# Three groups of weight units multiplied in pairs of ring slots, 512 columns a pass

## The chip, the cores and the metric

The kernel runs on one core of one Trainium2 chip. The metric is the device time in microseconds of one execution of the whole program, lower is better. Before the change it is 1397.33 us, the median of 3 runs (1395.53 to 1398.47).

## The reference

The reference is a small network on one sequence of 256 tokens with 1024 features, in float32. It has two parts, run one after the other.

The first part has two layers. Layer 0 is a sparse attention: a projection, an index score that picks 64 keys for each query, a softmax over the picked keys, an output projection. Layer 1 is a gated linear attention (GLA): `proj = x @ w_in` is split into q, k, v, r and a narrow gate input; the log decay is summed within chunks of 64 tokens; the output is the part within a chunk, from decayed q times k, plus a part from a running state. Behind each comes a layer norm, an MLP of 4096 hidden features with a squared ReLU, and a layer norm.

The second part projects its normed input to the inputs of four branches. One is a differential attention (a_q, a_k, a_v), one a forgetting attention (f_q, f_k, f_v), one a causal convolution of 31 taps, one a short convolution. Each is multiplied by its own branch matrix and gated, the sum goes through an output matrix, and a cross attention to a second input and a feed-forward block with a 3-tap convolution follow.

All that matters for the change are three of the projections: v of the GLA layer (1024 columns), a_v (512 columns) and f_v (512 columns). Each is `x @ w`, with x of 256 tokens by 1024 features.

## The kernel before

**Units and the ring.** All large weights are cut into 183 units of 128 partitions by 2048 floats (1 MB), in the order of their use (`UNITS`). GLA's v is `gv`, units 48 to 51; a_v is `av`, units 96 and 97; f_v is `fv`, units 102 and 103. A ring of `RING` = 4 slots holds them, unit u in slot u % 4. SyncE's queue loads a unit into `raw`. ScalarE copies it, rounded to the fp32r type, into `whi` (`high_part`, L906). VectorE writes the remainder into `wlo` (`low_part`, L1307). A product is then three matmuls into the same PSUM bank, high by high, high by low and low by high (`three`, L422 to L424). TensorE may begin a unit when its low part is there (`arrived`).

**Activations.** The input of a projection lies as features by tokens, in high and low parts `xh` and `xl`: 8 blocks of 128 features, 256 tokens each.

**Two kinds of unit.** In most units (`unit_up`) the weights are the stationary operand and the 256 tokens stream. For v-like projections (`unit_tok`, L463) the result is wanted as tokens by features, so the tokens are stationary and the weights stream. A unit holds 256 output features: for each half `t` of the tokens and each of the 8 feature blocks, three matmuls stream 256 columns of the unit, in all 48 matmuls. Both halves go into one bank `lin`, 256 columns each.

**Order and waits.** Each result bank has a number, a job, given out by `plan()`. `LAST[u]` is the last job that reads unit u. `bank(j)` waits until job j - 4 has been copied out of its bank. `high_part(u)` waits for the transfer of unit u and for job `LAST[u - 4]`. ScalarE's and VectorE's programs are written out in order. ScalarE's `copy(name, i, ...)` is `high_part` of the unit three further on (`AHEAD` = 3), a wait for the job, and the copy out of the bank (L921). VectorE's `next_low(name, i)` is `low_part` of the unit three further on.

**Around gv.** In front of gv TensorE computes the gate's low-rank input and the gate (L672, L679). ScalarE and VectorE turn that into the log decay and its running sum `bcum` (L1582 to L1590). VectorE's program then is:

```
            next_low("gv", 0)
            next_low("gv", 1)
            level_args(0)
            link(v.memset(attnD[:], 0.0))
            next_low("gv", 2)
            next_low("gv", 3)
            ...
            for l in range(6):
                level_pairs(l)
```

The product within a chunk is built in 7 levels. For each, VectorE makes the arguments (`level_args`, L1604 and L1605), ScalarE the exponential (`level_decay`, L1075), VectorE the decayed q and k (`level_pairs`, L1615), TensorE the product (`level`, L694), VectorE the sum. The units of `gr` are put between the levels on TensorE. Then come the transposes of k (L707), the states (L723) and the output.

**Around av and fv.** TensorE's order is aq, a narrow product, ak, av, fq, fk, fv, then c and s with steps of the two attentions between the units, all `unit_up` but av and fv. VectorE makes only low parts from ak to fv. From the first unit of s on it also computes the 31 taps of the convolution (L1746, L1748).

Of the kernel before, what the change touches and what calls it, by code (L numbers as in the profile page):

```python
# [17 lines left out]
P = 128  # L18
S = 256
D = 1024  # L20
DB = D // P
RING = 4
UT = 16
UW = UT * P
# [30 lines left out]
COUNT = dict(UNITS)  # L55
U0 = {}
# [10 lines left out]
def plan():  # L67


    job, last, n = {}, {}, [0]  # L70

    def add(name, i=0, unit=None, banks=1):
        job[name, i] = n[0]
        n[0] += banks
        if unit:
            last[U0[unit] + i] = n[0] - 1

    def units(name, count, banks=1):
        for i in range(count):
            add(name, i, name, banks)  # L80

    def norm(name, mean=False):
        if mean:
            add(name + "_mean")
        add(name + "_sq"); add(name + "_rstd")

    units("iq", 2); add("ik"); add("iw"); add("rope", 0); add("rope", 1); add("rope", 2)
    units("k", 1); units("v", 1); add("rope", 3)
    for i in range(6):
        add("idx", i)  # L90
    units("q", 4)
    for i in range(4):
        add("rope", 4 + i)
    units("ao", 4); norm("ln0", True)
    for layer in range(2):
        for half in range(2):
            units(f"up{layer}{half}", 8); units(f"dn{layer}{half}", 8)
        norm(f"ln{2 * layer + 1}", True)
        if layer == 0:
            units("gq", 2); units("gk", 2); add("alow"); add("gate_a", 0); add("gate_a", 1)  # L100
            units("gv", 4)
            for l in range(7):
                if l in GLA_FILL:
                    add(*GLA_FILL[l], GLA_FILL[l][0])
                add("level", l)
            add("gr", 2, "gr"); add("kd", 0); add("kd", 1); add("state", 0); add("state", 1)
            for i in range(4):
                add("gla_o", i)
            add("gr", 3, "gr")
            add("gla_sq"); add("gla_rstd", 0); add("gla_rstd", 1)  # L110
            units("go", 4); norm("ln2", True)
    norm("pre_mix")
    units("aq", 2); add("fg")
    for name in ("ak", "av", "fq", "fk", "fv", "c", "s"):
        units(name, COUNT[name])
    add("gate0", 0, "gate0"); add("gate0", 1, "gate0"); add("ya_sq"); add("gate0", 2, "gate0"); add("ya_rstd", 0); add("ya_rstd", 1)
    add("gate0", 3, "gate0"); units("br0", 2, 2); units("gate3", 4); units("br3", 2, 2)
    add("gate1", 0, "gate1"); add("gate1", 1, "gate1"); add("conv_mean"); add("gate1", 2, "gate1"); add("conv_sq")
    add("gate1", 3, "gate1"); add("conv_rstd"); units("br1", 2, 2); units("gate2", 4); units("br2", 2, 2)
    add("out", 0, "out"); add("out", 1, "out"); add("mem_sq"); add("out", 2, "out"); add("mem_rstd"); add("out", 3, "out")  # L120
    add("xk", 0, "xk"); add("post_mix_sq"); add("xk", 1, "xk"); add("post_mix_rstd"); add("xv", 0, "xv"); add("pre_x_sq"); add("xv", 1, "xv"); add("pre_x_rstd"); units("xq", 2); units("xo", 2, 2)
    norm("post_x"); norm("pre_ffn")
    units("fu", FB)
    for i in range(DB):
        add("fd", i)
    for u in range(COUNT["fd"]):
        last[U0["fd"] + u] = job["fd", (UT * u + UT - 1) // FB]
    norm("post_ffn")
    return job, last


JOB, LAST = plan()


# [47 lines left out]
def build(nc, units_d, x_d, mem_d, pos_d, vec_d, const_d, narrow_a_d, narrow_b_d, narrow_f_d, w_a2_d, b_fgt_d, lam_d, out_d):  # L182
    f32, f32r = mybir.dt.float32, mybir.dt.float32r
    i32 = mybir.dt.int32
    ACT, AX = mybir.ActivationFunctionType, mybir.AxisListType
    ctx = ExitStack()
    with ctx:
# [3 lines left out]
        def sbuf(name, shape, dt=f32, where=ctx):  # L191
            return where.enter_context(nc.sbuf_tensor(name, shape, dt))


        raw = [sbuf(f"raw{i}", [P, UW]) for i in range(RING)]
        whi = [sbuf(f"whi{i}", [P, UW], f32r) for i in range(RING)]
        wlo = [sbuf(f"wlo{i}", [P, UW], f32r) for i in range(RING)]
        h = sbuf("h", [P, DB, S])
        z = sbuf("z", [P, DB, S])
        xh = sbuf("xh", [P, DB, S], f32r)  # L200
# [210 lines left out]
        def _(pe):  # L411
# [41 lines left out]
            def unit_down(u, j, first, g=None):  # L453
# [6 lines left out]
                    last = three(o[:, 0, :], tile(u, k), (fh[:, k, :], fl[:, k, :]), k == 0, k == UT - 1)  # L460
                last.then_inc(job_done, 1)

            def unit_tok(u, j):  # L463

                arrived(u)
                o = bank(j)
                for t in range(2):
                    for k in range(DB):
                        at = slice(t * P, (t + 1) * P)
                        last = three(o[:, t, :], (xh[:, k, at], xl[:, k, at]), tile(u, 2 * k, 2), k == 0, k == DB - 1)  # L470
                last.then_inc(job_done, 1)
# [203 lines left out]
            for i in range(2):  # L675
# [2 lines left out]
                    hd = 2 * i + n  # L678
                    last = mm(o[:, n, :], w_a2[:, hd * P:(hd + 1) * P], alow[:], start=True, stop=True)  # L679
                last.then_inc(job_done, 1)  # L680
            for i in range(4):
                unit_tok(U0["gv"] + i, JOB["gv", i])

            def level(l):

# [76 lines left out]
                last = mm(o[0:8, 0, :], narrow_f[:, k, :], z[:, k, :], start=k == 0, stop=k == DB - 1)  # L762
            last.then_inc(job_done, 1)
            ups("ak")
            for i in range(2):
                unit_tok(U0["av"] + i, JOB["av", i])
            for name in ("fq", "fk"):
                ups(name)
            for i in range(2):
                unit_tok(U0["fv"] + i, JOB["fv", i])  # L770
            fill = [("c", i) for i in range(4)] + [("s", i) for i in range(6)]
            for s, (name, i) in enumerate(fill):
                unit_up(U0[name] + i, JOB[name, i])
# [117 lines left out]
        def _(act):  # L891
# [7 lines left out]
            def high_part(u, g=None, used=None):  # L899

                if u >= NU:
                    return
                act.wait_ge(raw_full[u % RING], per(16 * (u // RING + 1), g, 16))
                if u >= RING:
                    act.wait_ge(job_done, per(LAST[u - RING] + 1 if used is None else used, g, RING))
                f(whi[u % RING][:], raw[u % RING][:], ACT.Copy).then_inc(hi_ready, 1)  # L906

            def unit(name, i):

# [3 lines left out]
            def passed(name):  # L913

                for i in range(COUNT[name]):
                    high_part(U0[name] + i + AHEAD)

            def copy(name, i, dst, scale=1.0):
                unit(name, i)
                j = JOB[name, i]  # L920
                f(dst, lin[j % RING][:], ACT.Copy, scale=scale).then_inc(evac[j % RING], 1)  # L921
# [153 lines left out]
                f(decay[:], gtmp[:], ACT.Exp, scale=1.0 / 16).then_inc(lvl_exp, 1)  # L1075

            for i in range(4):
                copy("gv", i, gv_tok[:, :, i * S:(i + 1) * S])
                if i == 1:
                    level_decay(0)  # L1080
            for l in range(6):
# [47 lines left out]
            for i in range(2):  # L1129
                copy("ak", i, two(akT, i))  # L1130
            for i in range(2):
                copy("av", i, av_tok[:, :, i * S:(i + 1) * S])
            for name, dst in (("fq", fqT), ("fk", fkT)):
                for i in range(2):
                    copy(name, i, two(dst, i))
            for i in range(2):
                copy("fv", i, fv_tok[:, :, i * S:(i + 1) * S])

            def branch_split(n, src, ready):

# [143 lines left out]
        def _(dve):  # L1284
# [18 lines left out]
            def low_part(u, g=None):  # L1303

                if u < NU:
                    dve.wait_ge(hi_ready, per(u + 1, g, RING))
                    v.tensor_tensor(wlo[u % RING][:], raw[u % RING][:], whi[u % RING][:].bitcast(f32), ALU.subtract).then_inc(lo_ready, 1)  # L1307

            def next_low(name, i=None):

# [729 lines left out]
```

## Time and profile before

| | |
|---|---|
| median of the runs | 1397.33 us |
| the profiled execution, its own time | 1394.16 us |
| its span, first to last instruction | 1392.3 us |
| TensorE (PE) busy | 95% |
| VectorE (DVE) busy | 67% |
| ScalarE (ACT) busy | 45% |
| mean granted TensorE clock | 0.967 of full speed |

Times of the rows are microseconds from the start of the span. Matmuls are pipelined: each lasts longer than the distance to the next, so the distance between starts, and not the duration, is what one costs in a stream. PE is a matmul, PEld the load of its weights. A bracket at the end of a timeline row is the time that the engine idled before it, and what ended that. In a plain float32 product each matmul of the program appears as two records; in an fp32r product it is one.

### The profile page before, as it was taken

The numbers are of one execution on the slowest core, as the hardware profiler recorded it, in microseconds if no ns is written. First come the engines' busy times: TensorE is split into PE (matmuls) and PEld (weight loads), VectorE is DVE, ScalarE is ACT, GpSimd is POOL, SyncE is SP. The second block draws the span as 40 slices with busy tenths as digits, with TensorE's granted clock in tenths as the row PEclk, the third lists the DMA queues.
The fourth block names the chain that finished last, engine by engine and source line by source line (L and its number), as shares of the span: only waits on it lengthen the run. The fifth ranks groups of instructions, "written<-read, shape, count | busy, mean of one in ns | idle before, by whom it ended". The sixth has DMA issues, their size and how long they took to land.

```text
span 1392.3 us, 25125 instructions
## 1 busy us (share of the span) xinstructions
PE 1326.4 (95%) x10604; PEld 1272.3 (91%) x10604; DVE 928.1 (67%) x1448; ACT 627.4 (45%) x805; POOL 0.2 (0%) x4
## 2 busy tenths in 40 slices
PE   6889999999998899999999999999899999999897
PEld 6866999999998799999999999889898989999797
DVE  6783576466647767646665458888876665999943
ACT  5334454354444244534435444454445455555431
POOL 0000000000000000000000000000000000000000
PEclk9975999999999899999999999999999999999999
DMA  8320325545334133554532543334445241444430
GB/s 330 115 91 0 122 104 198 184 178 191 115 122 152 61 121 105 198 184 179 195 138 94 209 159 120 118 127 150 141 172 203 92 152 61 152 181 157 175 121 31
DMA packets 28361, 198.41 MB, mean 142 GB/s; under 512 B 3296, under 2 KB 3808, under 8 KB 4592
## 3 DMA queue, kind: packets, MB, share of 16 engines
q1 hardware_dynamic: 27072, 194.00, 38.7%
q10 hardware_dynamic: 1200, 3.14, 0.6%
q8 instruction: 66, 1.08, 0.3%
q14 instruction: 23, 0.19, 0.0%
HBM read 196.08 MB, written 1.05 MB: 142 GB/s over the span
## 4 chain that ended last, share of the span: by engine, by line
PE 69%; DVE 23%; ACT 3%; issue 3%; DMA 1%; DVEq 0%; ACTq 0%
PE lin L422 19%; PE lin L424 18%; PE lin L423 18%; DVE wlo L1307 7%; DVE conv L1748 3%; PE lin L504 2%; PE att L589 2%; PE att L497 2%; DVE fconv L1922 1%; PE att L556 1%; ACT whi L906 1%; PE att L573 1%; DVE fconv L1921 1%; DVE fconv L1923 1%; PE lin L527 1%
## 5 line engine op out<-in xcount | busy, mean ns | idle before, releaser
L422 PE MATMUL lin<-xh,whi 128*128 128x256 f32 x1936 | 556.2, 287 | 17.2 <-DVE xl L1317 11.8
L1307 DVE TENSOR_TENSOR wlo<-raw,whi 128x2048 fp32r<-128x2048 f32 x183 | 418.7, 2291 | 215.2 <-ACT whi L906 214.0
L423 PE MATMUL lin<-xl,whi 128*128 128x256 f32 x1936 | 550.8, 284 | 0.0
L424 PE MATMUL lin<-xh,wlo 128*128 128x256 f32 x1936 | 550.5, 284 | 0.0
L906 ACT ACTIVATE whi<-raw 128x2048 fp32r<-128x2048 f32 x183 | 348.5, 1906 | 179.5 <-PE lin L424 172.7
L422 PEld LDWEIGHTS lin<-xh,whi 128*128 128x128 f32 x1936 | 375.0, 194 | 21.4 <-DVE wlo L1307 10.6
L423 PEld LDWEIGHTS lin<-xl,whi 128*128 128x128 f32 x1936 | 375.0, 194 | 0.1
L424 PEld LDWEIGHTS lin<-xh,wlo 128*128 128x128 f32 x1936 | 374.5, 193 | 0.0
L422 PE MATMUL lin<-fh,whi 128*128 128x256 f32 x512 | 143.4, 280 | 0.0
L423 PE MATMUL lin<-fl,whi 128*128 128x256 f32 x512 | 142.8, 279 | 0.0
L424 PE MATMUL lin<-fh,wlo 128*128 128x256 f32 x512 | 142.8, 279 | 0.0
L424 PEld LDWEIGHTS lin<-fh,wlo 128*128 128x128 f32 x512 | 96.3, 188 | 0.0
L422 PEld LDWEIGHTS lin<-fh,whi 128*128 128x128 f32 x512 | 96.1, 188 | 0.0
L423 PEld LDWEIGHTS lin<-fl,whi 128*128 128x128 f32 x512 | 95.8, 187 | 0.0
L1748 DVE SCALAR_TENSOR_TENSOR conv<-upad,vec,conv 128x256 f32<-128x256 f32 x120 | 58.1, 484 | 3.9
L497 PE MATMUL att<-consts 128*128 128x128 f32 x464 | 57.0, 275 | 0.0
L422 PE MATMUL lin<-gh,whi 128*128 128x256 f32 x176 | 50.7, 288 | 6.4 <-DVE gl L1937 6.4
L497 PEld LDWEIGHTS att<-consts 128*128 128x128 f32 x464 | 54.6, 192 | 0.4 <-issue 0.2
L973 ACT ACTIVATE pr<-lg,nmax 128x128 f32<-128x128 f32 (+1 forms) x72 | 32.4, 452 | 48.5 <-DVE nmax L1436 43.5
L422 PE MATMUL lin<-whi,xh 128*128 128x256 f32 x176 | 50.7, 288 | 0.0
L423 PE MATMUL lin<-wlo,xh 128*128 128x256 f32 x176 | 50.5, 287 | 0.0
L424 PE MATMUL lin<-whi,xl 128*128 128x256 f32 x176 | 50.5, 287 | 0.0
(309 smaller groups left out, 1645.5 us busy)
## 6 DMA issues: line engine op xcount, KB each, us to landing
raw<-units_dram SPq DMA_DIRECT2D x183, 1024.0 KB, 4.8
h<-x_dram SPq DMA_DIRECT2D x1, 1024.0 KB, 6.8
memT<-mem_dram ACTq DMA_DIRECT2D x1, 1024.0 KB, 4.8
out_dram<-h SPq DMA_DIRECT2D x4, 256.0 KB, 2.0
consts<-consts_dram ACTq DMA_DIRECT2D x1, 867.5 KB, 12.2
narrow_a<-narrow_a_dram ACTq DMA_DIRECT2D x1, 544.0 KB, 14.1
vec<-vectors_dram ACTq DMA_DIRECT2D x1, 245.5 KB, 16.9
posi<-pos_dram ACTq DMA_DIRECT2D x1, 128.0 KB, 8.0
```

The lines of the kernel that those rows point to most:

```text
L422: mm(out, w[0], a[0], start=first, stop=False)
L423: mm(out, w[0], a[1], start=False, stop=False)
L424: return mm(out, w[1], a[0], start=False, stop=last)
L497: mm(att[0][:, 0:P], ident, ident, start=True, stop=True)
L504: ins = mm(flat[:, (col + t) * width:(col + t + 1) * width], block[:, t * P:(t + 1) * P], ones[:, 0:width], start=first and t == 0, stop=l ...
L527: last = mm(o[:, n, t * P:(t + 1) * P], inv[:, col:col + 1].broadcast_to([P, P]), ident, start=True, stop=True)
L556: last = mm(o, qT[r, i // 2, q], keys[r, i // 8, 0:w], start=True, stop=True)
L589: last = mm(o, v, pT[u % 2][:, n, :], start=b == 0, stop=b == att_keys(u, m) // P - 1)
L906: f(whi[u % RING][:], raw[u % RING][:], ACT.Copy).then_inc(hi_ready, 1)
L973: last = f(pr[u % 2][:, m, 0:w], lg[u % 2][:, m, 0:w], ACT.Exp, scale=-1.0, bias=nmax[:, u % 2, m:m + 1], accum_out=rsum[:, u % 2, m:m + 1])
L1307: v.tensor_tensor(wlo[u % RING][:], raw[u % RING][:], whi[u % RING][:].bitcast(f32), ALU.subtract).then_inc(lo_ready, 1)
L1748: ins = v.scalar_tensor_tensor(out=conv[:, b, :], in0=x, scalar=w, in1=conv[:, b, :], op0=ALU.mult, op1=ALU.add)
```

## The change

`unit_tok` for gv, av and fv becomes `units_tok`, which takes two neighbouring units at once. The slots of `whi` and of `wlo` become one tensor each, so that an operand can reach over two slots. For each half of the tokens, the 256 columns of the one unit and the 256 of the other stream in one matmul of 512 columns into a bank of its own. The bank of job j holds the first half of the tokens and 512 features, that of job j + 1 the second half. In `plan()` both units of a pair have the second job as their last. ScalarE copies a bank into the tensor of its half of the tokens. The units `v` and `xv` stay with `unit_tok`.

```diff
--- before.py
+++ after.py
@@ -79,6 +79,11 @@
         for i in range(count):
             add(name, i, name, banks)
+    def tokens(name, count):
+        for i in range(0, count, 2):
+            add(name, i); add(name, i + 1)
+            last[U0[name] + i] = last[U0[name] + i + 1] = n[0] - 1
+
     def norm(name, mean=False):
         if mean:
             add(name + "_mean")
@@ -98,7 +103,7 @@
         norm(f"ln{2 * layer + 1}", True)
         if layer == 0:
             units("gq", 2); units("gk", 2); add("alow"); add("gate_a", 0); add("gate_a", 1)
-            units("gv", 4)
+            tokens("gv", 4)
             for l in range(7):
                 if l in GLA_FILL:
                     add(*GLA_FILL[l], GLA_FILL[l][0])
@@ -112,7 +117,10 @@
     norm("pre_mix")
     units("aq", 2); add("fg")
     for name in ("ak", "av", "fq", "fk", "fv", "c", "s"):
-        units(name, COUNT[name])
+        if name in ("av", "fv"):
+            tokens(name, 2)
+        else:
+            units(name, COUNT[name])
     add("gate0", 0, "gate0"); add("gate0", 1, "gate0"); add("ya_sq"); add("gate0", 2, "gate0"); add("ya_rstd", 0); add("ya_rstd", 1)
     add("gate0", 3, "gate0"); units("br0", 2, 2); units("gate3", 4); units("br3", 2, 2)
     add("gate1", 0, "gate1"); add("gate1", 1, "gate1"); add("conv_mean"); add("gate1", 2, "gate1"); add("conv_sq")
@@ -193,8 +201,10 @@
         raw = [sbuf(f"raw{i}", [P, UW]) for i in range(RING)]
-        whi = [sbuf(f"whi{i}", [P, UW], f32r) for i in range(RING)]
-        wlo = [sbuf(f"wlo{i}", [P, UW], f32r) for i in range(RING)]
+        whi_ring = sbuf("whi", [P, RING, UW], f32r)
+        wlo_ring = sbuf("wlo", [P, RING, UW], f32r)
+        whi = [whi_ring[:, i, :] for i in range(RING)]
+        wlo = [wlo_ring[:, i, :] for i in range(RING)]
         h = sbuf("h", [P, DB, S])
         z = sbuf("z", [P, DB, S])
         xh = sbuf("xh", [P, DB, S], f32r)
@@ -460,6 +470,19 @@
                     last = three(o[:, 0, :], tile(u, k), (fh[:, k, :], fl[:, k, :]), k == 0, k == UT - 1)
                 last.then_inc(job_done, 1)
+            def units_tok(u, j):
+
+
+                for n in range(2):
+                    arrived(u + n)
+                at = u % RING
+                for t in range(2):
+                    o = bank(j + t)
+                    for k in range(DB):
+                        q, cols = slice(t * P, (t + 1) * P), slice(2 * k * P, (2 * k + 2) * P)
+                        last = three(o[:], (xh[:, k, q], xl[:, k, q]), (whi_ring[:, at:at + 2, cols], wlo_ring[:, at:at + 2, cols]), k == 0, k == DB - 1)
+                    last.then_inc(job_done, 1)
+
             def unit_tok(u, j):
                 arrived(u)
@@ -678,8 +701,8 @@
                     hd = 2 * i + n
                     last = mm(o[:, n, :], w_a2[:, hd * P:(hd + 1) * P], alow[:], start=True, stop=True)
                 last.then_inc(job_done, 1)
-            for i in range(4):
-                unit_tok(U0["gv"] + i, JOB["gv", i])
+            for i in (0, 2):
+                units_tok(U0["gv"] + i, JOB["gv", i])
             def level(l):
@@ -762,12 +785,10 @@
                 last = mm(o[0:8, 0, :], narrow_f[:, k, :], z[:, k, :], start=k == 0, stop=k == DB - 1)
             last.then_inc(job_done, 1)
             ups("ak")
-            for i in range(2):
-                unit_tok(U0["av"] + i, JOB["av", i])
+            units_tok(U0["av"], JOB["av", 0])
             for name in ("fq", "fk"):
                 ups(name)
-            for i in range(2):
-                unit_tok(U0["fv"] + i, JOB["fv", i])
+            units_tok(U0["fv"], JOB["fv", 0])
             fill = [("c", i) for i in range(4)] + [("s", i) for i in range(6)]
             for s, (name, i) in enumerate(fill):
                 unit_up(U0[name] + i, JOB[name, i])
@@ -903,7 +924,7 @@
                 act.wait_ge(raw_full[u % RING], per(16 * (u // RING + 1), g, 16))
                 if u >= RING:
                     act.wait_ge(job_done, per(LAST[u - RING] + 1 if used is None else used, g, RING))
-                f(whi[u % RING][:], raw[u % RING][:], ACT.Copy).then_inc(hi_ready, 1)
+                f(whi[u % RING], raw[u % RING][:], ACT.Copy).then_inc(hi_ready, 1)
             def unit(name, i):
@@ -914,6 +935,10 @@
                 for i in range(COUNT[name]):
                     high_part(U0[name] + i + AHEAD)
+
+            def two_tok(t, i):
+
+                return t[:, i % 2, 512 * (i // 2):512 * (i // 2) + 512].rearrange("p (a s) -> p a s", s=S)
             def copy(name, i, dst, scale=1.0):
                 unit(name, i)
@@ -1075,7 +1100,7 @@
                 f(decay[:], gtmp[:], ACT.Exp, scale=1.0 / 16).then_inc(lvl_exp, 1)
             for i in range(4):
-                copy("gv", i, gv_tok[:, :, i * S:(i + 1) * S])
+                copy("gv", i, two_tok(gv_tok, i))
                 if i == 1:
                     level_decay(0)
             for l in range(6):
@@ -1129,12 +1154,12 @@
             for i in range(2):
                 copy("ak", i, two(akT, i))
             for i in range(2):
-                copy("av", i, av_tok[:, :, i * S:(i + 1) * S])
+                copy("av", i, two_tok(av_tok, i))
             for name, dst in (("fq", fqT), ("fk", fkT)):
                 for i in range(2):
                     copy(name, i, two(dst, i))
             for i in range(2):
-                copy("fv", i, fv_tok[:, :, i * S:(i + 1) * S])
+                copy("fv", i, two_tok(fv_tok, i))
             def branch_split(n, src, ready):
@@ -1304,7 +1329,7 @@
                 if u < NU:
                     dve.wait_ge(hi_ready, per(u + 1, g, RING))
-                    v.tensor_tensor(wlo[u % RING][:], raw[u % RING][:], whi[u % RING][:].bitcast(f32), ALU.subtract).then_inc(lo_ready, 1)
+                    v.tensor_tensor(wlo[u % RING], raw[u % RING][:], whi[u % RING].bitcast(f32), ALU.subtract).then_inc(lo_ready, 1)
             def next_low(name, i=None):
```

## Rows read from the trace of the kernel before

**Rows 1.** The page, part 1: busy time of each engine.

```profile
PE 1326.4 (95%) x10604; PEld 1272.3 (91%) x10604; DVE 928.1 (67%) x1448; ACT 627.4 (45%) x805; POOL 0.2 (0%) x4
```

**Rows 2.** The page, part 4: the chain that ended last, by engine.

```profile
PE 69%; DVE 23%; ACT 3%; issue 3%; DMA 1%; DVEq 0%; ACTq 0%
```

**Rows 3.** The chain of waits in 760 to 816 us, by line.

```profile
by line: PE lin L422 33.4%; PE lin L424 33.2%; PE lin L423 33.0%; PE att L559 0.8%
```

**Rows 4.** Timeline, ScalarE, av: start, duration, instruction, idle before and its releaser.

```profile
769.05 0.60 ACT L921 ACTIVATE gate<-lin 128x512 f32<-128x512 f32 x1 [3.36 <-PE lin L424]
...
774.81 0.60 ACT L921 ACTIVATE gate<-lin 128x512 f32<-128x512 f32 x1 [3.36 <-PE lin L424]
```

**Rows 5.** The chain of waits in 740 to 960 us: start, duration, piece.

```profile
841.42 0.45 PE att L559 x4
...
843.50 0.42 DVE conv L1746
```

**Rows 6.** Timeline, TensorE, from gv's first matmul on.

```profile
404.05 0.39 PE L422 MATMUL lin<-whi,xh 128*128 128x256 f32 x1
...
404.39 0.27 PE L424 MATMUL lin<-whi,xl 128*128 128x256 f32 x1
404.50 0.28 PE L422 MATMUL lin<-whi,xh 128*128 128x256 f32 x1
...
405.57 0.41 PE L423 MATMUL lin<-wlo,xh 128*128 128x256 f32 x1
...
408.13 0.41 PE L423 MATMUL lin<-wlo,xh 128*128 128x256 f32 x1
```

**Rows 7.** Timeline, TensorE, two of the GLA levels.

```profile
430.50 1.15 PE L694 MATMUL lin<-qk 128*64 128x64 f32 x32 [1.68 <-DVE qk L1615]
...
442.48 1.93 PE L694 MATMUL lin<-qk 128*64 128x64 f32 x32 [3.80 <-DVE qk L1615]
```

**Rows 8.** The chain of waits in 396 to 500 us.

```profile
429.16 1.28 DVE qk L1615 x2
...
460.47 3.68 PE lin L694 x64
```

**Rows 9.** Timeline, VectorE, gv and the first levels.

```profile
416.04 4.49 DVE L1307 TENSOR_TENSOR wlo<-raw,whi 128x2048 fp32r<-128x2048 f32 x2
...
424.74 4.50 DVE L1307 TENSOR_TENSOR wlo<-raw,whi 128x2048 fp32r<-128x2048 f32 x2 [1.92 <-ACT whi L906]
429.16 0.68 DVE L1615 TENSOR_TENSOR qk<-gkT,decay 128x512 f32<-128x512 f32 x1
...
438.20 2.29 DVE L1307 TENSOR_TENSOR wlo<-raw,whi 128x2048 fp32r<-128x2048 f32 x1 [2.92 <-ACT whi L906]
```

**Rows 10.** Timeline, TensorE, two groups of plain fp32 matmuls with what follows them.

```profile
24.55 3.61 PE L606 MATMUL lin<-h,narrow_a 128*128 128x256 f32 x16
28.00 0.62 PE L611 MATMUL lin<-narrow_a,h 128*128 128x8 f32 x5
...
491.71 3.68 PE L504 MATMUL lin<-consts,z 128*128 128x64 f32 x32
495.23 0.89 PE L497 MATMUL att<-consts 128*128 128x128 f32 x6
```

**Rows 11.** Timeline, VectorE, low parts of units 97 and 98.

```profile
759.49 4.50 DVE L1307 TENSOR_TENSOR wlo<-raw,whi 128x2048 fp32r<-128x2048 f32 x2 [1.38 <-ACT whi L906]
```

**Rows 12.** Timeline, ScalarE, gv: high parts of 51, 52, 54 and 55, copy of 49.

```profile
410.92 1.90 ACT L906 ACTIVATE whi<-raw 128x2048 fp32r<-128x2048 f32 x1
...
413.20 1.90 ACT L906 ACTIVATE whi<-raw 128x2048 fp32r<-128x2048 f32 x1
417.35 0.60 ACT L921 ACTIVATE gv_tok<-lin 128x512 f32<-128x512 f32 x1 [2.24 <-PE lin L424]
...
425.02 1.90 ACT L906 ACTIVATE whi<-raw 128x2048 fp32r<-128x2048 f32 x1
...
436.27 1.89 ACT L906 ACTIVATE whi<-raw 128x2048 fp32r<-128x2048 f32 x1
```

## The prediction

> **What bounds the kernel now.** I read the page first. TensorE has matmuls in flight for 95% of the span, and the chain that ended last is 69% TensorE and 23% VectorE [rows 1, 2]. That is an average, so the second view is the timeline around each place that the diff touches, and the two kinds of place differ.
>
> Around av and fv the chain of waits is matmuls alone, 99.6% of it on the three lines of `three` [rows 3]. ScalarE copies one result after another at 769.05 and 774.81, each time after 3.36 us of idling for TensorE [rows 4]: 5.76 us a unit, over 48 matmuls 0.120 us each. TensorE is the bound, and what it saves there is carried on. The chain stays with TensorE until 841.42 and then goes to VectorE's convolution taps, which start after an attention step that TensorE releases [rows 5]. A TensorE that is earlier at 815 therefore brings the taps forward too.
>
> Around gv it is different. TensorE has matmuls in flight from 404.05 [rows 6] to 428.8, but behind them VectorE runs the GLA levels, and TensorE waits for it: 1.68 us before the first level, 3.80 us before a later one [rows 7]. From 429.16 on the chain is VectorE and ScalarE; TensorE takes it over only at 460.47 [rows 8]. So in that stage the VectorE work that starts at 429.16 [rows 9] sets the end.
>
> **The change, part by part.**
>
> *Streaming.* For 8 units, 384 matmuls of 256 columns become 192 of 512. The columns stay the same, half of the weight loads go. What is a pass of 512 worth? No 512-column matmul of this type is in the trace, so I bound it. At the full clock 256 columns take 0.120 us. At the low clock (1.2 GHz) twelve of them take 408.13 - 405.57 = 2.56 us, 0.2133 each, which is 256 columns at 1.2 GHz and nothing over [rows 6]. So at 2.4 GHz streaming needs 0.1067, and 0.0133 comes from elsewhere. A cost added to every matmul would show at the low clock too; a floor under it would not. Two plain-fp32 groups speak for a floor of the weight load: 32 matmuls of 64 columns with 128-column weights come every (495.23 - 491.71) / 32 = 0.110 us although they stream half as long as the others, and 16 that stream 256 columns at half rate (0.2133 of streaming) come every (28.00 - 24.55) / 16 = 0.2156 [rows 10]. A load of 128 weight columns is hidden behind 0.21 us of streaming but for 0.002. A 512-column pass streams for just as long. I take 0.2156: 48 x (2 x 0.120 - 0.2156) = 1.17 us less for each pair at the full clock. The ends: 0.2133 (streaming alone, 1.28 a pair) and 0.240 (no gain); a load that is serial after all gives 0.2267 (0.64).
>
> The Trainium skill, "TensorE: Matmul & The Clock Gate" (Back-to-back issue gap), gives N / 2.4 + 2.5 ns for a matmul by itself. For 512 columns it is 215.8 ns, and rows 10 agree. For 256 columns it is 109.2 ns, and the trace disagrees with 120. By the page alone a pair would save 48 x (218.4 - 215.8) ns = 0.12 us, and the change would have next to no gain; the measured 0.120 decides.
>
> *av and fv.* Two pairs, 2 x 1.17 = 2.3 us off the path, if nothing new is waited for. The first matmul of a pair now needs both units. For av the second unit's low part is the first of the two that start at 759.49 and take 4.50 together: ready at 761.8, wanted at 763.3 (one unit before 769.05), so no wait [rows 4, 11]. For fv the margin is wider: ScalarE makes the high part of a unit right behind the copy of the unit four before it. Both ring slots come free at the pair's end instead of one in its middle; ScalarE then has two high parts (1.90 each) and a copy before the next unit's 5.76 us are over, and the unit after next is the first that needs one. So no matmul waits. VectorE's low part behind fv may reach into the first attention step; it lies beside the next unit's 5.76 us of TensorE, and uncovered it would cost its 2.29 us once. -2.3.
>
> *gv, first pair* (units 48, 49). It starts at 404.05 as now; both are ready. The low clock holds for about 3.4 us of it, where a wide pass gains nothing. Of 96 matmuls about 80 run at the full clock: 40 x 0.0244 = 1.0 us less. Unit 49's copy starts at 417.35 now [rows 12], so the pair ends at 416.4.
>
> *gv, second pair* (units 50, 51). It needs the low part of 51. That is the first of two at 416.04, 2.25 us: 418.3 [rows 9]. VectorE comes to it from the gate's chain, and 51's high part was long made (410.92 + 1.90 [rows 12]), so TensorE's speed doesn't move it. Today unit 50 fills that time. Now TensorE stands still from 416.4 to 418.4, about 2.0 us, and gives back all of the first pair's gain and more. The pair then takes 48 x 0.2156 + 0.3 (first gap and tail) = 10.65 us: 429.0, where unit 51 ends at 428.8 now.
>
> *The ring.* High part of unit u waits for the last matmul on unit u - 4. For 52 that was unit 48's end, now the first pair's: ScalarE starts it at 416.5 instead of 413.20 and VectorE's low part of 52 begins 0.2 us later. Small. For 54 it was unit 50's end, which let ScalarE start at 425.02 [rows 12]; now it is the second pair's, 429.1. Its high part ends at 431.0. And VectorE's program has the low part of 54 in front of `level_pairs(0)`: everything of the levels is queued behind it. Low part 431.1 to 433.3, and the first level starts at 433.3 instead of 429.16: **+4.1 us** on the chain that sets this stage.
>
> Is that absorbed further on? VectorE idles 2.92 us before its low part at 438.20 [rows 9], which looks like slack. It waits there for ScalarE's high part at 436.27, which comes straight behind a `decay` that waits for VectorE's own level arguments [rows 9, 12]: the wait moves with the chain. TensorE idles some 5.5 us before level 0 instead of 1.68, which costs it the clock as the 3.80 us at 442.48 did (32 matmuls of a level in 1.93 us there, 1.15 at 430.50 [rows 7]). About 0.8 us there and up to 1.7 in the unit behind; both have room beside VectorE. +4.1 stays.
>
> *Sum.* +4.1 - 2.3 = +1.8 us. On the profiled execution's own 1394.16 us that is 1396.0. The median of the runs shown is 3.2 us above that execution, so I put it on the median: 1397.33 + 1.8 = 1399.1.
>
> **The rivals.**
>
> *A, no faster streaming.* What holds 256 columns at 0.120 is the feed of the moving operand (0.469 ns a column), not the weight load. Then 512 take 0.240. For it: at the low clock a feed of that rate would be hidden as well, and fp32's floor (0.110) is not quite 0.120. Against it: a burst's first matmuls come closer than 0.120 (404.39 to 404.50 [rows 6]). Price: no gain at av and fv; gv's first pair still waits out 418.4, the second ends at 418.4 + 11.52 + 0.3 = 430.2, the levels start at 434.5. +5.3: 1402.6, slower. Each pass of the second pair, of av and of fv counts, 144 in all, so it decides from 0.2225 on (1.8 + 144 x 0.0069 = 2.8 us, which is 0.2%). The serial load (0.2267) lies between: 1.8 + 144 x 0.0111 = +3.4: 1400.7.
>
> *B, the clock falls in the new stall.* 2.0 us of standing still at 416.4. For it: the clock is at half by 405.57 although TensorE had matmuls from 404.05 on [rows 6]. Against it: after 1.68 us of idling at 430.50 the level ran at full clock [rows 7], while 3.80 us did cost it. At half clock for 3.4 us the second pair takes 1.7 us more: +3.5, 1400.8.
>
> *C, the delay of unit 54 does not reach the end.* Then only av and fv are left: -2.3, 1395.0. For it: VectorE has idle time in the level stage. Against it: each of those waits ends at ScalarE work that follows VectorE's own. Since 2.3 us is 0.16%, it too would hardly be told from no change.
>
> **How the numbers follow.** A measurement of this kernel tells 0.2% (2.8 us) from no change, hardly less. Chances: forecast 0.56 (1399.1, give or take 1.0, from where the low-clock stretches fall), A 0.17 and the serial load 0.05, B 0.09, C 0.13. Slower by over 0.2%: A, most of B and of the serial load (0.11), and 0.08 of the forecast's upper side: 0.36. Faster by over 0.2%: a part of C, 0.06. The rest, 0.58, within. The range reaches from C to A: 1395.0 to 1402.8.
>
> **What would show it.** Right: the 192 wide passes start every 0.215 to 0.217 us; TensorE idles about 2 us between the gv pairs, ended by the low part of 51; ScalarE's high part of 54 starts after gv's last matmul; VectorE's first level starts some 4 us later against the start of gv, and TensorE idles over 5 us before level 0; from ak to c the time shrinks by 2.3 us. Wrong: passes every 0.240 (A); wide passes at half clock behind the stall (B); the stretch from gv's first matmul to the `state` matmuls no longer than before (C); or any new wait in front of av or fv.

## The result, and the profile after

The changed kernel takes 1399.82 us (median of 20 runs, 1397.27 to 1404.37), the kernel before 1395.81 us (20 runs, 1392.27 to 1398.47). The ratio is 1.0029, interval [1.0022, 1.0037]: slower by 4.0 us, with 3.1 to 5.2 from the interval. The prediction said 1399.1 and +1.8. That the time was met to 0.7 us is luck: the three runs shown before lay 1.5 us above the median of twenty. The direction and the place held; the difference was over twice as large.

On the page little tells the two apart but the count of matmuls: 192 fewer, in nearly the same busy time [rows 1, 2].

```profile
PE 1327.2 (95%) x10412; PEld 1263.2 (90%) x10412; DVE 927.9 (66%) x1448; ACT 627.7 (45%) x805; POOL 0.2 (0%) x4
...
PE 70%; DVE 23%; ACT 3%; issue 3%; DMA 1%; DVEq 0%; ACTq 0%
```

The timeline of TensorE around gv (`three` is now L432 to L434, the level L717) answers to [rows 6, 7]:

```profile
405.83 0.50 PE L432 MATMUL lin<-whi,xh 128*128 128x512 f32 x1
...
416.62 0.39 PE L434 MATMUL lin<-whi,xl 128*128 128x512 f32 x1
420.22 0.47 PE L432 MATMUL lin<-whi,xh 128*128 128x512 f32 x1 [3.21 <-DVE wlo L1332]
...
421.71 0.63 PE L434 MATMUL lin<-whi,xl 128*128 128x512 f32 x1
...
423.85 0.63 PE L433 MATMUL lin<-wlo,xh 128*128 128x512 f32 x1
...
425.09 0.39 PE L434 MATMUL lin<-whi,xl 128*128 128x512 f32 x1
...
432.57 0.39 PE L434 MATMUL lin<-whi,xl 128*128 128x512 f32 x1
438.55 1.76 PE L717 MATMUL lin<-qk 128*64 128x64 f32 x27 [5.59 <-DVE qk L1640]
```

Three things are to be seen. The stall between the pairs is there and is ended by the low part of unit 51. Behind it the clock falls: from 421.71 to 423.85 five passes take 2.14 us, 0.428 each. The windows of the same stretch (from and to, length, TensorE busy and count, granted clock, DMA share, GB/s) show it directly:

```profile
417.00:420.22 3.22, 0.01 (x1) 1.00 0.00 0
420.22:421.30 1.08, 1.08 (x5) 0.91 0.38 68
421.30:424.30 3.00, 3.00 (x9) 0.50 0.93 336
```

At the full clock 33 passes take 432.57 - 425.09 = 7.48 us, 0.2267 each: not 0.2156. ScalarE (its high parts are L927) answers to [rows 12], VectorE (low parts L1332, first level L1640) to [rows 9]:

```profile
417.10 1.91 ACT L927 ACTIVATE whi<-raw 128x2048 fp32r<-128x2048 f32 x1 [2.01 <-PE lin L434]
...
433.06 1.91 ACT L927 ACTIVATE whi<-raw 128x2048 fp32r<-128x2048 f32 x1 [4.90 <-PE lin L434]
```

```profile
417.83 4.49 DVE L1332 TENSOR_TENSOR wlo<-raw,whi 128x2048 fp32r<-128x2048 f32 x2
...
426.52 2.29 DVE L1332 TENSOR_TENSOR wlo<-raw,whi 128x2048 fp32r<-128x2048 f32 x1 [1.92 <-ACT whi L927]
435.00 2.29 DVE L1332 TENSOR_TENSOR wlo<-raw,whi 128x2048 fp32r<-128x2048 f32 x1 [6.18 <-ACT whi L927]
437.21 0.69 DVE L1640 TENSOR_TENSOR qk<-gkT,decay 128x512 f32<-128x512 f32 x1
```

High parts of 52 and 54 start as TensorE ends a pair. Before, the low parts of 53 and 54 were one row of 4.50 us. Now 6.18 us of idling stand between them, and the first level is queued behind the second.

Since the two executions differ by 1.78 us already where gv starts, stages are compared by distances. The columns are: first gv matmul to VectorE's first level; from there to the first `state` matmul; first narrow product behind aq to the first logits of the second part (this holds av and fv); from there to the end of the span; gv's first matmul to the end. Each is a difference of starts in the timelines.

| kernel | to first level | levels | av, fv | rest | gv to end | ratio to before |
|---|---|---|---|---|---|---|
| before | 25.11 | 43.90 | 67.08 | 577.33 | 988.29 | 1 |
| changed | 31.38 | 42.98 | 65.84 | 577.34 | 992.36 | 1.0029 [1.0022, 1.0037] |
| e1_av_fv | 25.12 | 42.66 | 65.85 | 577.20 | 985.67 | 0.9982 [0.9973, 0.9991] |
| e2_gv | 31.39 | 42.88 | 67.08 | 579.95 | 996.12 | 1.0040 [1.0026, 1.0054] |
| e3_late54 | 22.90 | 44.12 | 65.85 | 578.55 | 986.24 | 0.9975 [0.9965, 0.9985] |
| e4_before_late54 | 22.89 | 43.50 | 67.08 | 579.97 | 988.30 | 0.9981 [0.9972, 0.9990] |
| e5_early51 | 26.31 | 43.73 | 65.85 | 578.28 | 989.02 | 0.9995 [0.9986, 1.0004] |
| e6_pairs_both | 23.62 | 43.20 | 65.85 | 576.22 | 983.72 | 0.9968 [0.9956, 0.9980] |
| e7_before_both | 20.59 | 43.01 | 67.09 | 580.05 | 985.58 | 0.9968 [0.9956, 0.9980] |
| e8_av_fv_both | 20.60 | 43.30 | 65.85 | 578.33 | 982.92 | 0.9960 [0.9947, 0.9973] |

The stretch from the states to the narrow product is 274.8 to 274.9 us in all. "Levels" differs by 1.2 us between before and e1_av_fv, "rest" by up to 3.8 us between all, each time with the same code in it.

In "levels" the reason is where a stretch at half clock ends. Before, it reaches into the last unit of `gr`; in the changed kernel that unit runs at the full clock as a whole (48 matmuls). Before, then changed:

```profile
456.20:466.50 10.30, 7.67 (x107) 0.50 0.12 52
466.50:471.00 4.50, 4.50 (x40) 1.00 0.01 4
```

```profile
462.10:472.30 10.20, 5.76 (x97) 0.50 0.28 105
472.30:478.00 5.70, 5.70 (x48) 1.00 0.00 0
```

In "rest" the sum of the time at half clock is not the reason: e7_before_both has about 12 us of it in 580.05, e6_pairs_both about 23 us in 576.22. Most of what e6_pairs_both gains there, 2.4 us, falls in its last 64 us, and the clock is full in both of the following stretches. In the units of the last feed-forward block 24 passes of 256 columns take 2.82 us before (0.1175 each) and 2.72 us in e6_pairs_both (0.1133 each), with the same code; there are 528 such passes, so 0.0042 each is 2.2 us:

```profile
1362.33 0.28 PE L422 MATMUL lin<-gh,whi 128*128 128x256 f32 x1
...
1365.15 0.28 PE L422 MATMUL lin<-gh,whi 128*128 128x256 f32 x1
```

```profile
1358.67 0.28 PE L432 MATMUL lin<-gh,whi 128*128 128x256 f32 x1
...
1361.39 0.28 PE L432 MATMUL lin<-gh,whi 128*128 128x256 f32 x1
```

Why is not known. So single-profile totals are worth some 3 us. The third column is sharp. The first is as sharp for most kernels: before has half clock in gv's first matmuls and e1_av_fv has none, and both take 25.1. For e6_pairs_both it is not, as is shown below.

For the changed kernel the columns add up: +6.27, -0.92, -1.24, and the rest 0.0 give the +4.1 of the profiled execution, and the medians differ by 4.0. That the rest is equal to 0.01 us in these two profiles is luck, as the other rows show.

### The profile page after: what moved, and what is told of

The parts are those of the page before. It is cut to its first block, busy times and chain, and to the rows that moved or that the text cites. A ratio compares the mean times of both kernels' runs of the same rounds, so it can differ in the third digit from the quotient of the medians.

```text
span 1398.2 us, 24737 instructions
## 1 busy us (share of the span) xinstructions
PE 1327.2 (95%) x10412; PEld 1263.2 (90%) x10412; DVE 927.9 (66%) x1448; ACT 627.7 (45%) x805; POOL 0.2 (0%) x4
## 4 chain that ended last, share of the span: by engine, by line
PE 70%; DVE 23%; ACT 3%; issue 3%; DMA 1%; DVEq 0%; ACTq 0%
PE lin L432 19%; PE lin L434 19%; PE lin L433 19%; DVE wlo L1332 6%; DVE conv L1773 3%; PE lin L527 2%; PE att L612 2%; PE att L520 2%; DVE fconv L1947 1%; PE att L579 1%; PE att L596 1%; ACT whi L927 1%; DVE fconv L1946 1%; DVE fconv L1948 1%; PE lin L550 1%
## 5 line engine op out<-in xcount | busy, mean ns | idle before, releaser
L432 PE MATMUL lin<-xh,whi 128*128 128x256 f32 x1936 | 556.5, 287 | 17.3 <-DVE xl L1342 11.8
L1332 DVE TENSOR_TENSOR wlo<-raw,whi 128x2048 fp32r<-128x2048 f32 x183 | 418.8, 2291 | 221.1 <-ACT whi L927 219.8
L434 PE MATMUL lin<-xh,wlo 128*128 128x256 f32 x1936 | 550.8, 285 | 0.0
L927 ACT ACTIVATE whi<-raw 128x2048 fp32r<-128x2048 f32 x183 | 348.6, 1906 | 196.4 <-PE lin L434 189.4
L432 PEld LDWEIGHTS lin<-xh,whi 128*128 128x128 f32 x1936 | 375.3, 194 | 21.6 <-DVE wlo L1332 10.7
L434 PEld LDWEIGHTS lin<-xh,wlo 128*128 128x128 f32 x1936 | 374.8, 194 | 0.0
L432 PE MATMUL lin<-fh,whi 128*128 128x256 f32 x512 | 143.4, 280 | 0.0
L434 PE MATMUL lin<-fh,wlo 128*128 128x256 f32 x512 | 142.8, 279 | 0.0
L434 PEld LDWEIGHTS lin<-fh,wlo 128*128 128x128 f32 x512 | 96.3, 188 | 0.0
L432 PEld LDWEIGHTS lin<-fh,whi 128*128 128x128 f32 x512 | 96.1, 188 | 0.0
L432 PE MATMUL lin<-gh,whi 128*128 128x256 f32 x176 | 50.7, 288 | 6.4 <-DVE gl L1962 6.4
L433 PE MATMUL lin<-gl,whi 128*128 128x256 f32 x176 | 50.3, 286 | 0.0
L434 PE MATMUL lin<-gh,wlo 128*128 128x256 f32 x176 | 50.1, 285 | 0.0
L432 PE MATMUL lin<-whi,xh 128*128 128x512 f32 (+1 forms) x112 | 39.5, 352 | 3.2 <-DVE wlo L1332 3.2
```

The source lines that it names most:

```text
L432: mm(out, w[0], a[0], start=first, stop=False)
L433: mm(out, w[0], a[1], start=False, stop=False)
L434: return mm(out, w[1], a[0], start=False, stop=last)
L927: f(whi[u % RING], raw[u % RING][:], ACT.Copy).then_inc(hi_ready, 1)
L1332: v.tensor_tensor(wlo[u % RING], raw[u % RING][:], whi[u % RING].bitcast(f32), ALU.subtract).then_inc(lo_ready, 1)
```

## The experiments

**e1_av_fv: pairs for av and fv alone.** The edit puts gv back to single units:

```diff
-            tokens("gv", 4)
+            units("gv", 4)
-            for i in (0, 2):
-                units_tok(U0["gv"] + i, JOB["gv", i])
+            for i in range(4):
+                unit_tok(U0["gv"] + i, JOB["gv", i])
-                copy("gv", i, two_tok(gv_tok, i))
+                copy("gv", i, gv_tok[:, :, i * S:(i + 1) * S])
```

> Only av and fv go in pairs; gv is as in the kernel before. Theory (serial load: a wide pass costs 0.2267 us instead of 0.240): 96 wide passes x 0.0133 = 1.3 us faster than before. Rival 1 (weight load hidden, 0.2156): 2.3 us faster. Rival 2 (no faster streaming, 0.240): no change, and then the whole 4 us of the change would be gv's in another split. In the trace the stretch from the narrow product behind aq (fg) to the first attention logits is 67.08 us before; theory 65.8, rival 1 64.7, rival 2 67.1.

Measured: the stretch is 65.85, 1.23 us shorter, so the theory's 1.3 and not the 2.3 of a hidden load. The kernel is faster than before: 0.9982, 2.5 us (1.3 to 3.8). In the profile 1.2 is the stretch, and another 1.2 lies in the levels (42.66 against 43.90 for the same code), where the half clock ended earlier. These are the rows from which the stretch is read, of the kernel before, then of the changed one:

```profile
747.93 2.33 PE L762 MATMUL lin<-z,narrow_f 128*8 128x256 f32 x10
...
815.01 0.49 PE L559 MATMUL att<-gate,aqT 64*128 64x128 f32 x4
```

```profile
755.01 2.33 PE L785 MATMUL lin<-z,narrow_f 128*8 128x256 f32 x10
...
820.85 0.49 PE L582 MATMUL att<-gate,aqT 64*128 64x128 f32 x4
```

TensorE is busy for the whole of it in both, at the full clock, with 96 matmuls fewer:

```profile
747.93:815.01 67.08, 67.08 (x545) 1.00 0.48 173
```

```profile
755.01:820.85 65.84, 65.84 (x449) 1.00 0.44 161
```

**e2_gv: pairs for gv alone.** The same edit, mirrored, for av and fv.

> Only gv goes in pairs; av and fv are as in the kernel before. Theory (low part of 54 gated by the second pair's end, with a pass of 0.2267): the first level starts 4.7 us later against gv's first matmul, 6.3 if the clock falls in the stall between the pairs; 5.3 us slower than before in the median, give or take 1. Rival (the delay is made up again before the states): under 2 us slower. It and the run with av and fv alone should add up to the change's +4.0.

Measured: first level at 31.39 (theory 4.7 or, with the clock, 6.3 later: it is 6.28), ratio 1.0040, +5.6 us (3.6 to 7.5). The rival is out. All of the loss is gv's. With e1_av_fv it adds up to +3.1, where the change has +4.0; the intervals are wide enough for that.

**e3_late54 and e4_before_late54: unit 54's parts behind the levels' start.** The edit, the same in both kernels; gv's last copy goes with the high part:

```diff
 # ScalarE
-            for i in range(4):
+            for i in range(3):
                 copy("gv", i, ...)
                 if i == 1:
                     level_decay(0)
             for l in range(6):
                 if l < 5:
                     level_decay(l + 1)
+                if l == 0:
+                    copy("gv", 3, ...)
 # VectorE
             next_low("gv", 2)
-            next_low("gv", 3)
 ...
+                if l == 1:
+                    next_low("gv", 3)
                 if l in GLA_FILL:
                     next_low(*GLA_FILL[l])
```

> The changed kernel, but unit 54's high part and the copy of gv's last bank stand behind the second level's exponential on ScalarE, and 54's low part behind the third level's arguments on VectorE, where it idles. Theory (the loss is the level stage queued behind 54's low part): the first level starts at about 23 us after gv's first matmul instead of 31.4, the time falls by 5 to 7 us against the changed kernel and is 2 to 3 us below the kernel before. Rival (the loss is TensorE's stall between the pairs and the clock that it costs): TensorE still stalls 2 to 3 us, so the time falls by at most 1 us against the changed kernel and stays 3 us above before.

> Control: the same move of unit 54's parts, in the kernel before (no pairs). Theory: VectorE's first level starts at 427.1 instead of 429.16, 1.5 to 2 us faster than before; then e3_late54 against this one shows the pairs without the queue behind 54: about 1 us faster for it (1.3 from av and fv). Rival (the stall between the pairs costs by itself): e3_late54 is 1 to 2 us slower than this one.

Measured: 0.9975 for the changed kernel with the move, 3.5 us below before (2.1 to 4.9) and so 7.5 below the changed one (1.0029 - 0.9975 = 0.54%), a little more than the theory's 5 to 7. The first level starts at 22.90, as in the control at 22.89. TensorE still stands still for 3.19 us between the pairs, and the half clock behind that is there too:

```profile
420.44 0.47 PE L432 MATMUL lin<-whi,xh 128*128 128x512 f32 x1 [3.19 <-DVE wlo L1335]
```

The stall is there and the loss is gone: the queue behind 54's low part was the way by which it reached the levels. In e3_late54 VectorE begins the level first and makes 54's low part (435.25) among the next levels:

```profile
428.95 0.68 DVE L1643 TENSOR_TENSOR qk<-gkT,decay 128x512 f32<-128x512 f32 x1
...
435.25 2.29 DVE L1335 TENSOR_TENSOR wlo<-raw,whi 128x2048 fp32r<-128x2048 f32 x1 [0.18 <-ACT whi L927]
438.47 2.29 DVE L1335 TENSOR_TENSOR wlo<-raw,whi 128x2048 fp32r<-128x2048 f32 x1 [0.94 <-ACT whi L927]
```

The control gains 2.7 us (1.4 to 3.9) by the same move without any pair, more than the 1.5 to 2 expected. The pairs then add 0.8 by the ratios and 0.1 by the medians, both inside the intervals; e3_late54 is not the 1 to 2 us slower that the rival wanted.

**e5_early51: unit 51 before the gate's chain.** In the changed kernel (the copy of gv's first bank then no longer makes 51's high part):

```diff
 # ScalarE, behind the copy of alow
+            high_part(U0["gv"] + 3)
 # VectorE, behind the gate's bias
+            low_part(U0["gv"] + 3)
             dve.wait_ge(softplus, 1)
 ...
-            next_low("gv", 0)
             next_low("gv", 1)
```

> The changed kernel, but the high and the low part of unit 51 are made before the gate's chain, where ScalarE and VectorE idle behind TensorE (about 402 and 405 us); 54's parts stay where they are. Theory (both the stall of TensorE and the queue behind 54's low part, which starts at the second pair's end, are in the loss): no stall between the pairs, no fall of the clock behind it, the second pair ends some 22 us after gv's first matmul instead of 27.2, and the first level starts at 26.4 instead of 31.4: 4 to 5 us faster than the changed kernel, within 1 us of the kernel before. Rival (VectorE's own chain sets the first level, so the stall costs nothing): under 1 us faster than the changed kernel.

Measured: first level at 26.31 (theory 26.4), ratio 0.9995, 4.7 us below the changed kernel. Nothing is between the pairs any more, both run at the full clock, and the low part of 54 starts at 429.89 instead of 435.00:

```profile
429.89 2.29 DVE L1337 TENSOR_TENSOR wlo<-raw,whi 128x2048 fp32r<-128x2048 f32 x1 [2.01 <-ACT whi L927]
432.10 0.68 DVE L1646 TENSOR_TENSOR qk<-gkT,decay 128x512 f32<-128x512 f32 x1
```

So the stall matters through the queue only: it makes the second pair's end later, and 54's parts wait for that end. Either end of the link can be cut, here the stall, in e3_late54 the queue. What e5_early51 does not tell apart is the stall and the half clock behind it: both go together.

**e6_pairs_both, e7_before_both, e8_av_fv_both: both moves, in the changed kernel, in the kernel before, and with pairs for av and fv alone.** The edits are the two above.

> The changed kernel with both moves (51's parts early, 54's parts late). Theory: the first level starts at about 22 us after gv's first matmul, the whole is 1 us faster than e3_late54 and 3 to 5 us faster than before. Rival (behind the removed queue the level stage is bound by its own VectorE chain): the same as e3_late54, within 0.5 us.

> Control: both moves in the kernel before, no pairs. Theory: 3 to 4 us faster than before, and e6_pairs_both is ahead of it by the 1.3 us of av and fv only, since the gv pairs give nothing where VectorE is the bound.

> Pairs for av and fv alone, gv by single units, and both moves. Theory: the fastest of all, 4 to 5 us below the kernel before; against e7_before_both it shows the 1.3 us of 96 wide passes again. Rival (gv's pairs are worth something once nothing queues behind them): e6_pairs_both is faster than this one by up to 1.3 us.

Measured: e6_pairs_both has its first level at 23.62, not 22. The 1.6 us between are the clock. In its profile the first pair of gv runs at half clock for 3.3 us, and in e5_early51, which makes 51's parts at the same place, it does not (e6_pairs_both, then e5_early51):

```profile
406.20:409.50 3.30, 3.30 (x9) 0.52 0.13 20
```

```profile
405.80:417.00 11.20, 11.20 (x50) 1.00 0.28 95
```

The first pair's end releases the high part of unit 52, and that starts 12.90 us after gv's first matmul (405.00) in e6_pairs_both and 11.28 us after it in e5_early51 (417.07 and 405.79). All that follows up to the low part of unit 53 keeps this distance of 1.6.

The link is the ring again. Unit 52's high part (the ScalarE row) needs the first pair's end, and 52's low part (the VectorE row) stands in front of the first level's arguments:

```profile
417.90 1.92 ACT L927 ACTIVATE whi<-raw 128x2048 fp32r<-128x2048 f32 x1 [4.90 <-PE lin L434]
```

```profile
419.92 2.29 DVE L1340 TENSOR_TENSOR wlo<-raw,whi 128x2048 fp32r<-128x2048 f32 x1 [3.06 <-ACT whi L927]
422.13 0.68 DVE L1638 TENSOR_TENSOR gtmp<-bcum 128x512 f32<-128x512 f32 x1
```

In e8_av_fv_both VectorE reaches that low part with no idling. So pairs in gv put the first level 3.0 us later even with both moves (23.62 against 20.59), and of these 1.6 are the half clock and 1.4, an estimate from these rows, the coarser release of the slots. With single units a half clock in the same place costs nothing there: e7_before_both has it and takes 20.59, e8_av_fv_both has none and takes 20.60.

By the ratios e6_pairs_both and e7_before_both are level, both at 0.9968 (2.8 to 6.1 us below before). The 1.3 us expected between them is neither shown nor excluded by intervals of that width, and the 983.72 of e6_pairs_both holds the 2.4 us of faster passes in its last 64 us. For the same reason the total does not decide between theory and rival for e6_pairs_both against e3_late54: the ratios put it 1.0 us ahead, gv and levels together 0.2 (66.82 against 67.02).

e8_av_fv_both has the lowest median of all, 1390.66 us, 0.9960 [0.9947, 0.9973] of before. Its interval overlaps those of the two others, so that it is the fastest of the three rests on the first and the third column: 86.45 us together, against 87.68 in e7_before_both and 89.47 in e6_pairs_both. That it beats both the kernel before and the changed kernel does not.

**w128, w384, w64: what a pass costs.** Of these only the distance between starts is read; each ran once (1491.70, 1394.48 and 1400.89 us, the kernel before beside them 1396.41). w384 leaves out the last 64 columns of each unit, w64 half of the tokens, so both do less work than the kernel must.

```diff
 # w128, in unit_tok: two passes of 128 for each of 256
-                        last = three(o[:, t, :], ..., tile(u, 2 * k, 2), ...)
+                        last = three(o[:, t, c * P:(c + 1) * P], ..., tile(u, 2 * k + c), ...)
 # w384, in units_tok
+                        cols = slice(2 * k * P, 2 * k * P + 192)
+                        last = three(o[:, :, 0:192], ...)
 # w64, in units_tok
+                        q = slice(t * P, t * P + 64)
+                        last = three(o[0:64], ...)
```

> The kernel before, with all the v-like units (v, gv, av, fv, xv) streamed in passes of 128 columns instead of 256. Only the distance between starts is read. At 256 and 512 columns it is 0.1200 and 0.2267 us, streaming plus 0.0133. Theory S (a fixed 0.0133 added to every pass): 0.0533 + 0.0133 = 0.067 us. Theory F (the load of 128 weight columns is a floor, as in the prediction): 0.110 us. If neither, the addition depends on the width.

> The changed kernel, with passes of 384 columns: two times 192, the last 64 of each unit's 256 columns are left out. Theory S (0.0133 added to every pass): 0.160 + 0.0133 = 0.173 us between starts. Theory M (something that the pass of 512 alone pays, since it fills a bank or reaches over two slots): 0.162 to 0.167 us.

> The changed kernel, with 64 of the 128 tokens of each half as stationary operand (the other half of the tokens is left out), passes of 512 columns. Theory L (the 0.0133 is the part of the weight load that is not hidden, and goes by its columns): 0.2133 + 0.0067 = 0.220 us between starts. Theory S (fixed for each fp32r pass, whatever its weights): 0.2267 as in the changed kernel.

Measured, each between two rows of the same line at the full clock. w128, 18 passes in 2.00 us, 0.111:

```profile
828.02 0.27 PE L422 MATMUL lin<-whi,xh 128*128 128x128 f32 x1
...
830.02 0.28 PE L422 MATMUL lin<-whi,xh 128*128 128x128 f32 x1
```

w384, 12 passes in 2.08 us, 0.1733:

```profile
798.67 0.33 PE L432 MATMUL lin<-whi,xh 128*128 128x384 f32 x1
...
800.75 0.33 PE L432 MATMUL lin<-whi,xh 128*128 128x384 f32 x1
```

w64, 6 passes in 1.38 us, 0.230:

```profile
812.12 0.40 PE L432 MATMUL lin<-whi,xh 128*64 128x512 f32 x1
...
813.50 0.40 PE L432 MATMUL lin<-whi,xh 128*64 128x512 f32 x1
```

At 128 columns theory F fits: there is a floor of 0.111, near fp32's 0.110 [rows 10]. From 256 on theory S fits: 0.1200, 0.1733, 0.2267 are the columns at 2.4 GHz (0.1067, 0.1600, 0.2133) plus 0.0133 each. Halving the stationary columns does not make the addition smaller. It makes it larger, 0.0167 (0.230), which neither theory had; theory L, that it is the unhidden part of the weight load, is out. Nor is the addition one number for all passes of 256 columns: it is 0.0133 in the projections, but 0.0108 and 0.0067 in the two stretches of the feed-forward block shown above (0.1175 and 0.1133). So 0.0133 is what the passes of this change cost, not a rule for every pass, and what sets it is open.

## Why the prediction was right and wrong

- **The queue behind unit 54** was right, and shown: +4.1 predicted, 6.27 measured at the first level, gone when 54's parts are moved (e3_late54), and down to 1.2 when the stall is taken away (e5_early51).
- **The stall between the pairs** was right in kind: 3.21 us, not 2.0. The half-clock stretch that slowed gv's first matmuls in the profile of before was not there in the profile after, so the first pair ended earlier and waited longer for the same low part of 51 (its wait ends 14.39 us after gv's first matmul; predicted was 14.35). The length of the stall is not a price by itself.
- **Rival B, the clock falling in the stall**, had 0.09 and happened, in the profiled executions of the changed kernel, of e2_gv and of e3_late54. It was one of the prediction's own signs of being wrong. From 421.3 to 424.3 the granted clock is 0.50; eight passes at 0.427 instead of 0.227 are 1.6 us. The 1.68 us of idling that had not cost the clock [rows 7] was too weak a witness for 3.2.
- **The wide pass** was mis-sized: 0.2156 taken, 0.2267 measured. The step that failed is "A cost added to every matmul would show at the low clock too". It does not: at the low clock 256 columns take 0.2133 and 512 take 0.428, next to nothing over, and at the full clock there is 0.0133 on the passes of 256, 384 and 512 columns in these projections. The plain-fp32 rows [rows 10] were read rightly but carry over to fp32r only for the floor. The measured price stood in the sentence on the serial load, at +3.4 and a chance of 0.05, with another mechanism behind it, which w64 speaks against. For av and fv: 1.24 us measured, 2.3 predicted, 1.28 by 0.0133. In gv's second pair it costs 48 x 0.0111 = 0.5 us. The Trainium skill, "TensorE: Matmul & The Clock Gate" (Back-to-back issue gap), gives N / 2.4 + 2.5 ns, 215.8 ns for 512 columns. The trace disagrees: 226.7 measured. That rows 10 agree, as the prediction says, holds for the time alone: they have no pass of 512 columns, but plain fp32 ones of 256 that stream as long.
- **The sum redone**: 4.1 + 0.5 + 1.6 = 6.2 to the first level (6.27), less 0.9 in the levels (where the half clock ended earlier), less 1.24: +4.1. The 1.8 of the forecast missed 0.5, 1.6 and 1.1 of these and did not have the 0.9.
- **Rival A** (0.240) is refuted by the rows. **Rival C** is refuted by its own sign: from gv's first matmul to the states it is 74.36 us, 5.3 more than before, and e2_gv is slower by 5.6 in all.
- **Nothing waits at av and fv** was right: TensorE is busy throughout, and the stretch shrinks by the passes' own gain in every kernel that has the pairs.

## What to carry to other kernels

Taking two ring slots at once doubles the grain of their release. Look for the first instruction that needs a released slot, and for what is written behind it in the program of that engine: here a gain of 0.0133 us on each of 192 passes stood against a stage of 43 us that began 6 us later. A saving on TensorE is worth having only where the chain of waits is matmuls (av and fv), and the cheapest gain, 2.7 us without any pair, lay in the order in which the programs of ScalarE and VectorE take a conversion that nobody needs yet. Before a single profile is compared with another by stages, compare where the half clock falls in each: it moved one and the same stage by 1.6 us here, and only in the kernels in which that stage hangs on TensorE.

## What the runs showed of the hardware

In the v-like projections an fp32r pass at the full clock costs its columns at 2.4 GHz plus 0.0133 us for 256, 384 and 512 columns, and 0.111 at 128. At half clock the addition is not seen (0.2133 for 256, 0.428 for 512). What it is stays open. With 64 instead of 128 stationary columns a pass of 512 takes 0.230; plain fp32 that streams for 0.2133 us has hardly any of it (0.2156, [rows 10]); and other passes of 256 columns come every 0.1175 us, in one profile every 0.1133 (e6_pairs_both).

Where the half-clock stretches fall differs from one execution's profile to another's. It moved "levels" by 1.2 us for the same code, and the first level by 1.6 us in e6_pairs_both. "Rest" differs by up to 3.8 us, of which 2.4 are the passes of 0.1133; what the clock has in the remainder was not worked out.
